# Two neighbouring heads, one in each half of the TensorE array and each with its own PSUM bank, in the attentions of a three-layer hybrid model

## The reference

```python
# window attention, per block of 128 queries
scores = jnp.einsum('bnqkgd,bnskd->bnkgqs', qb, kb).astype(jnp.float32) * (HEAD_DIM ** -0.5)
scores = jnp.where(mask[None, :, None, None], scores, -jnp.inf)
probs = jax.nn.softmax(jnp.concatenate([scores, sink], axis=-1), axis=-1)[..., :-1]

# forgetting attention, per block of 128 queries
cum = jnp.transpose(jnp.cumsum(log_f, axis=1), (0, 2, 1))
sc = jnp.einsum('bqhd,bkhd->bhqk', q[:, start:end], k[:, :end]).astype(jnp.float32) * scale
sc = sc + cum[:, :, start:end, None] - cum[:, :, None, :end]
sc = jnp.where(causal[None, None], sc, -jnp.inf)
probs = jax.nn.softmax(sc, axis=-1).astype(v.dtype)
```

## Time and profile before

| | us |
|---|---|
| median of 3 runs | 2251.22 |
| lowest and highest | 2249.53 and 2251.26 |
| the profiled execution | 2250.25 |
| its span | 2248.5 |
| TensorE busy | 2045.1 |
| VectorE busy | 1519.9 |
| ScalarE busy | 1106.0 |
| GpSimd busy | 90.9 |

### The profile page before, as it was taken

One profiled execution on the slowest core, in us unless ns is written; L12 is line 12 of the kernel. 1 busy time (PEld: TensorE's weight loads), 2 busy tenths in 40 slices (PEclk: granted clock), 3 DMA queues, 4 the chain that ended last, 5 costly groups with the idle time before them and its releaser, 6 DMA issues.

```text
span 2248.5 us, 25347 instructions
## 1 busy us (share of the span) xinstructions
PE 2045.1 (91%) x9466; PEld 1579.8 (70%) x9466; DVE 1519.9 (68%) x2305; ACT 1106.0 (49%) x1672; POOL 90.9 (4%) x85
## 2 busy tenths in 40 slices
PE   5998999998899999997689789876999999999996
PEld 4776777776777777776545445535888888888885
DVE  4967555555586845546846766326888888888885
ACT  4544545444453445444321012115777777777774
POOL 0000000000000000000002100001000000000000
PEclk9999999999899999998899899997999999999998
DMA  6533434344443443433444322253999999998994
GB/s 196 158 124 103 141 113 122 103 141 153 125 147 117 139 116 104 125 106 116 134 138 149 97 87 94 72 183 136 330 328 331 331 329 331 327 330 328 331 330 150
DMA packets 134602, 411.08 MB, mean 183 GB/s; under 512 B 17464, under 2 KB 19128, under 8 KB 107344
## 3 DMA queue, kind: packets, MB, share of 16 engines
q1 hardware_dynamic: 128480, 407.25, 53.9%
q0 software_dynamic: 6000, 2.22, 0.4%
HBM read 406.21 MB, written 19.45 MB: 189 GB/s over the span
## 4 chain that ended last, share of the span: by engine, by line
PE 76%; DVE 17%; ACT 4%; issue 2%; DMA 1%; SPq 0%; DVEq 0%; ACTq 0%; POOLq 0%
PE bank L588 17%; PE bank L589 16%; PE bank L590 16%; PE bank L636 9%; DVE r L1043 5%; DVE w_lo L1043 4%; PE bank L933 3%; PE bank L567 2%; PE bank L704 2%; PE bank L781 1%; PE bank L807 1%; PE bank L687 1%; PE bank L874 1%; DVE r L1049 1%; DVE r L1046 1%
## 5 line engine op out<-in xcount | busy, mean ns | idle before, releaser
L1043 DVE TENSOR_TENSOR w_lo<-w_raw,w_hi 128x1024 fp32r<-128x1024 f32 (+1 forms) x372 | 445.7, 1217 | 244.2 <-ACT w_hi L1875 235.6
L1875 ACT CAST w_hi<-w_raw 128x1024 fp32r<-128x1024 f32 (+1 forms) x266 | 277.8, 1047 | 187.6 <-PE bank L590 187.5
L588 PE MATMUL bank<-w_hi,h_hi 128*128 128x512 f32 x800 | 327.8, 410 | 12.9 <-DVE w_lo L1043 12.8
L589 PE MATMUL bank<-w_lo,h_hi 128*128 128x512 f32 x800 | 316.1, 395 | 0.0
L590 PE MATMUL bank<-w_hi,h_lo 128*128 128x512 f32 x800 | 315.7, 395 | 0.0
L588 PEld LDWEIGHTS bank<-w_hi,h_hi 128*128 128x128 f32 x800 | 153.4, 192 | 48.8 <-DVE w_lo L1043 14.1
L2031 ACT ACTIVATE r<-bank,small 128x256 f32<-128x256 f32 (+1 forms) x152 | 63.8, 424 | 243.2 <-DVE small L1046 243.1
L590 PEld LDWEIGHTS bank<-w_hi,h_lo 128*128 128x128 f32 x800 | 152.6, 191 | 33.7
L589 PEld LDWEIGHTS bank<-w_lo,h_hi 128*128 128x128 f32 x800 | 153.3, 192 | 29.5
L1043 DVE TENSOR_TENSOR w_lo<-r,w_hi 128x1024 fp32r<-128x1024 f32 x106 | 129.1, 1246 | 44.2 <-ACT w_hi L2140 44.1
L636 PE MATMUL bank<-w_raw,h_all 128*128 128x512 f32 (+1 forms) x320 | 142.3, 601 | 1.1 <-DVE h_all L1043 1.1
(11 more groups left out here) (320 smaller groups left out, 4125.7 us busy)
## 6 DMA issues: line engine op xcount, KB each, us to landing
w_raw<-in_w_in SPq DMA_DIRECT2D x236, 512.0 KB, 3.6
r<-in_w_up SPq DMA_DIRECT2D x69, 1024.0 KB, 5.2
w_raw<-in_w_gate SPq DMA_DIRECT2D x68, 1024.0 KB, 5.1
w_raw<-in_w_down SPq DMA_DIRECT2D x36, 1024.0 KB, 5.2
r<-in_w_down SPq DMA_DIRECT2D x34, 1024.0 KB, 5.1
w_raw<-in_w_proj SPq DMA_DIRECT2D x48, 512.0 KB, 3.7
w_raw<-in_w_out SPq DMA_DIRECT2D x24, 512.0 KB, 3.9
w_raw<-in_w_mem_kv SPq DMA_DIRECT2D x8, 512.0 KB, 3.6
```

The source lines that it names most:

```text
L588: e.matmul(out_, sh, mh, start=first, stop=False, skip_group_check=shared)
L589: e.matmul(out_, sh, ml, start=False, stop=False, skip_group_check=shared)
L1043: o.did(v.tensor_tensor(out_, a, b, op), sem, value)
L1875: a.copy(halves(n)[0], raw_of(n)).then_inc(w_hi, 1)
```

## The change

A unit is now heads h and h+1, so one head is in each half of the array. Each head's scores have a bank of their own, always 4 and 5 (`score_banks`); the turned probabilities always take 6 (`turn_bank`). `scores` is cut in two: `products`, for both heads, then `rest`, for the first and then the second head. The sum of forget gates runs over all 128 rows: `picks` is now zero from row 64 on, so the second copy of `cum` adds nothing. The banks are one tensor, so that VectorE can take the maximum of both banks by one instruction; ScalarE releases each bank behind its own exponential. The memory attention has no rest and only changes its banks.

```diff
+UNITS, UNITS_DSA, UNITS_MEM = ([(t, h) for t in range(T) for h in range(0, n, 2)] for n in (HEADS, 8, 4))
...
+        bank_all = ctx.enter_context(nc.psum_tensor("bank", [P, 8 * CH], F32))
+        banks = [bank_all[:, i * CH:(i + 1) * CH] for i in range(8)]
...
+            score_banks, turn_bank = Banks([4, 5]), Banks([6])
...
-                        b, bank = take(work, ("sc", tag, i))
+                        got = [take(score_banks, ("sc", tag, i, j)) for j in range(2)]
+                        last = [products(h0 + j, t, got[j][1][:, 0:keys], rest is None) for j in range(2)]
+                        if rest is not None:
+                            last = [rest(h0 + j, t, got[j][1][:, 0:keys]) for j in range(2)]
                         for j in range(2):
-                            done = scores(h0 + j * hs, t, bank[:, j * keys:(j + 1) * keys])
-                        done.then_inc(full[b], 1)
+                            last[j].then_inc(full[got[j][0]], 1)
                     if 1 <= i <= len(units):
                         t, h0 = units[i - 1]
                         n = 2 * keys_of(t) // P
-                        await_drained(("sc", tag, i - 1))
+                        for j in range(2):
+                            await_drained(("sc", tag, i - 1, j))
                         p = p_buf[(i - 1) % 2]
-                        b, bank = take(work, ("pt", tag, i - 1))
+                        b, bank = take(turn_bank, ("pt", tag, i - 1))
...
-                def scores(h, t, dst):
+                def products(h, t, dst, alone):
                     keys, par = (t + 1) * P, HD * (h % 2)
-                    e.matmul(dst, qT[par:par + HD, h // 2, t * P:(t + 1) * P], kT_c[par:par + HD, h // 2, 0:keys], start=True, stop=False)
-                    e.matmul(dst, picks[par:par + 64, h:h + 1].to_broadcast([64, P]), cum[par:par + 64, 0:keys], start=False, stop=False)
+                    return e.matmul(dst, qT[par:par + HD, h // 2, t * P:(t + 1) * P], kT_c[par:par + HD, h // 2, 0:keys], start=True, stop=alone)
+
+                def rest(h, t, dst):
+                    e.matmul(dst, picks[:, h:h + 1].to_broadcast([P, P]), cum[:, 0:(t + 1) * P], start=False, stop=False)
                     return e.matmul(dst[:, t * P:(t + 1) * P], idbf[:, :], causal_mask, start=False, stop=True)
...
+                        for j in range(2):
+                            await_full(("sc", tag, i, j))
                         c = t * heads + h0
-                        mx = mx_all[:, c:c + hs + 1:hs]
-                        o.did(v.tensor_reduce(mx, bank[:, 0:2 * keys_of(t)].rearrange("p (h k) -> p h k", h=2), AX, MAX))
+                        mx = mx_all[:, c:c + 2]
+                        two = bank_all[:, 4 * CH:6 * CH].rearrange("p (h k) -> p h k", h=2)
+                        o.did(v.tensor_reduce(mx, two[:, :, 0:keys_of(t)], AX, MAX))
...
                         for j in range(2):
-                            done = a.activation(p_buf[i % 2][:, j * keys:(j + 1) * keys], bank[:, j * keys:(j + 1) * keys], ACT.Exp,
-                                                bias=mx_all[:, c + j * hs:c + j * hs + 1], accum_out=sum_all[:, c + j * hs:c + j * hs + 1])
-                        done.then_inc(drained[b], 1)
+                            b, bank = await_full(("sc", tag, i, j))
+                            a.activation(p_buf[i % 2][:, j * keys:(j + 1) * keys], bank[:, 0:keys], ACT.Exp,
+                                         bias=mx_all[:, c + j:c + j + 1], accum_out=sum_all[:, c + j:c + j + 1]).then_inc(drained[b], 1)
...
-    c[:, 1250:1266] = i[:, None] % 32 == np.arange(16)
+    c[:, 1250:1266] = (i[:, None] % 32 == np.arange(16)) & (i[:, None] < 64)
```

More of the change, by code:

```diff
@@ L667, in dense, with attention @@
                         yield
-            def attention(tag, units, heads, dv, hs, keys_of, scores, v_of, p_buf, pT_buf):
+            def attention(tag, units, heads, dv, keys_of, products, rest, v_of, p_buf, pT_buf):
                 per_bank = min(CH // dv, heads)
@@ L777, in window @@
                 await_drained(("kT", l, 1))
-                def scores(h, t, dst):
+                def products(h, t, dst, alone):
                     keys, par = (t + 1) * P, HD * (h % 2)
-                    e.matmul(dst, qT[par:par + HD, h // 2, t * P:(t + 1) * P], kT_b[par:par + HD, h // KVH, 0:keys], start=True, stop=False)
+                    return e.matmul(dst, qT[par:par + HD, h // 2, t * P:(t + 1) * P], kT_b[par:par + HD, h // KVH, 0:keys], start=True, stop=alone)
+                def rest(h, t, dst):
                     return e.matmul(dst, idbf[:, :], causal_mask if t == 0 else window_mask, start=False, stop=True)
-                yield from attention(("b", l), UNITS, HEADS, HD, 2, lambda t: (t + 1) * P, scores,
+                yield from attention(("b", l), UNITS, HEADS, HD, lambda t: (t + 1) * P, products, rest,
                                      lambda h, b: kvb[:, b, 256 + (h // 4) * HD:256 + (h // 4 + 1) * HD],
@@ L856, in memory, with products @@
                 await_drained(("kTm", 1))
-                def scores(h, t, dst):
-                    return e.matmul(dst, qT_m[:, h, t * P:(t + 1) * P], kT_m[:, h, :], start=True, stop=True)
-                yield from attention("mem", UNITS_MEM, 4, 128, 1, lambda t: S, scores, lambda h, b: kmv[:, b, CH + h * 128:CH + (h + 1) * 128],
+                def products(h, t, dst, alone):
+                    return e.matmul(dst, qT_m[:, h, t * P:(t + 1) * P], kT_m[:, h, :], start=True, stop=alone)
+                yield from attention("mem", UNITS_MEM, 4, 128, lambda t: S, products, None, lambda h, b: kmv[:, b, CH + h * 128:CH + (h + 1) * 128],
                                      [R[9][:, 0:CH], R[9][:, CH:2 * CH]], [R[9][:, 2 * CH:3 * CH], R[9][:, 3 * CH:4 * CH]])
@@ L1284, in rope, with attention @@
                 o.prev()
-            def attention(tag, units, heads, dv, hs, keys_of, before, y3, stats_of, sink=None, gated=False):
+            def attention(tag, units, heads, dv, keys_of, y3, stats_of, sink=None, gated=False):
                 mx_all, sum_all = stats_of
@@ L1323, in finish @@
                 else:
-                    await_drained(("sc", tag, unit))
+                    for j in range(2):
+                        await_drained(("sc", tag, unit, j))
                 o.did(v.reciprocal(sm, sm))
@@ L1356, in window @@
                 await_drained(((("zb", l), 1), 1))
[L1357 removed]
+                yield from attention(("b", l), UNITS, HEADS, HD, lambda t: (t + 1) * P, y_b, att["b"], sink=sinks, gated=True)
                 yield
@@ L2018, in mamba, with attention @@
                 yield
-            def attention(tag, units, heads, dv, hs, keys_of, p_buf, pT_buf, stats_of, sink=False):
+            def attention(tag, units, heads, dv, keys_of, p_buf, pT_buf, stats_of, sink=False):
                 mx_all, sum_all = stats_of
```

42 lines of the change are left out of this document (18 added, 24 removed).

## The result

| | before | changed |
|---|---|---|
| median, us | 2251.24 | 2228.24 (2225.9 to 2229.79) |
| ratio to before | | 0.9899, 95% interval 0.9885 to 0.9913 |
| span of the profiled execution | 2248.5 | 2228.0 |

A forecast was written before the change was run, and what follows sets the result against it. TensorE was taken to bound the attention stages. Unit savings of 16 x 2.38 = 38.1 us, with +0.3 and +0.2 given back, took 2250.25 to 2212.7, or 2213.5 as median; range 2206 to 2229, forecast's chance 0.75.

The forecast's parts named there:

- The products of two halves overlap: Score products: two heads' products, one in each half, cost what one costs, 0.63 us at 256 keys, 0.42 at 128.
- Rival A: Score products: second head's first matmul does not pass first head's second; 10.9 us more, 2224 us; chance 0.09.
- Rival B: Score products: the halves do not overlap, only switches are saved; 20.8 us more, 2234 us; chance 0.05.
- Window units: Window attention, up to the turning: 0.54 us at 128 keys, saving 0.52; 0.87 at 256 keys, saving 0.72.
- mask to mask as before a turning: Step between a unit's two masks, without a trace row: booked at 0.06 and 0.12 us, bounds 0.05 and 0.16.
- the gate sum keeps its 0.06 and 0.12: Forget units: a gate sum over 128 rows costs as over 64, 0.06 us at 128 keys, 0.12 at 256.
- This margin does not shrink: Ahead of a unit's products: slack after the previous unit's exponential, 0.98 us at the tightest, stays, so waits cost nothing.
- rival C: Dense pieces come closer and wait for VectorE or ScalarE, or exponentials are late: at most 20 us back, 2218 to 2234; chance 0.07.
- Turnings have bank 6 alone and wait for the copy ..., a wait that stood behind them already: Turnings wait for the copy of the unit before, claimed to be no new wait; no size given.
- plus 0.2 to 0.5: Transposes of y_b in layer 0's forget stage: their first group meets the exponential wait instead of the second, costing 0.2 to 0.5 us.
- +0.2, bounds -3 and +3: Last stage's sparse and memory attention: gains of lone units and losses of pairs net to +0.2 us, bounds -3 and +3.
- I am wrong if the rows show the starts together and the span is not shorter by over 30 us: The prediction's own failure test: products of both heads start together, yet the span shortens by no more than 30 us.

The follow-up runs named there:

- Experiment 1: Changed kernel with the old choice of heads, h and h+2, both in the same half of the array: 2253.63 us, ratio 1.0004 to the kernel before.
- experiment 5: Changed kernel with both gate sums of a forget unit ahead of both masks, sums still over 128 rows: 2223.14 us, ratio 0.9883 to the kernel before.
- experiment 3: Changed kernel with gate sums over the 64 rows of the head's own half, between products and masks: 2223.35 us, ratio 0.9869 to the kernel before.
- experiment 7: Kernel before with only the fixed banks, scores in 4 and 5 in turn, turned weights in 6: 2257.44 us, ratio 1.0019.
- experiment 6: Changed kernel with gate sums over 64 rows and the third layer's attentions as before the change: 2220.2 us, and 2216.1 when run again.
- experiment 2: Changed kernel with each head's rest straight behind its product (product, rest, product, rest): 2281.87 us, ratio 1.0134 to the kernel before.

## Why the prediction was right, and where its sizes were off

- **The products of two halves overlap: right.** 0.64 for four instructions, 0.007 us between the heads. Experiment 1 takes the overlap away, and 18.5 of the 27.4 us gained in the first two layers go with it. Rival A would have put the second head's first product behind the first head's second, 0.3 later; the Trainium skill's rule behind it, "TensorE: Matmul & The Clock Gate", Part 3 ("The mechanism"), that matmuls start in program order, is contradicted here by a second kind of work beside the indexer's. Rival B is experiment 1, not this kernel.
- **Window units, "0.42 + 0.06 + 0.06" and "0.63 + 0.12 + 0.12": right.** Saved 0.51 and 0.73 a unit, 19.8 us over both layers. The bound "mask to mask as before a turning" held: 0.066 and 0.119.
- **Forget units: the term "the gate sum keeps its 0.06 and 0.12" failed.** At full height a gate sum takes 0.16 and 0.22 to its mask (mean of the two heads); the step from a mask to a gate sum, booked at 0.11, takes 0.04. Together 0.13 and 0.12 a unit, 4.0 us. Counting columns alone was the mistake. They are the same, and with its weights loaded ahead a full-height sum of 256 columns does take 0.12 (experiment 5's second); but behind the products, and behind a mask, the load over all rows no longer runs ahead (experiments 3 and 5).
- **"This margin does not shrink": true ahead of the products, false elsewhere.** No unit of the two stages waits there. But I read margins on TensorE's queue and only for the exponential. The window's last turning (1.19 us of wait), the one product with the values that waits for VectorE to empty bank 7 (0.57 of wait, 0.74 of delay) were within reach of a TensorE that runs 9 us ahead of VectorE's dense work. The window stages should have shortened by 9.9 each; they shortened by 8.0 and 7.6. Of the 4.2 us that are missing these two waits, in both layers, hold 2 x (1.19 + 0.74) = 3.9. That is rival C at a small size, which I had given 0.07 as a case of its own, where it is a cost that comes on top of the forecast.
- **"Turnings have bank 6 alone and wait for the copy ..., a wait that stood behind them already": wrong by 0.45 us in this place** (the copy ends after both exponentials), and free at the old length of a unit (experiment 7).
- **y_b's transposes, "plus 0.2 to 0.5" in layer 0:** 0.98 us of wait for the exponential became 1.58, and layer 1, which I had left out, went from 1.0 to 1.84, there for the copy. With 0.2 and 0.1 more for `y_lo` behind it, 1.7 us against 0.3.
- **The third layer, net "+0.2, bounds -3 and +3":** the mechanism was right (first pair: second scores 3.2 us behind the first, 3.0 forecast), the size 1.2 us by the waits, 2.4 by all profiles with the clock's share in it, 6.3 in the first comparison. The first two lie within the bounds. What I had no term for is the clock.

My own test was "I am wrong if the rows show the starts together and the span is not shorter by over 30 us". They do and it is not, so by it the sum was wrong. Its terms, put right: the net 37.6 less 4.0 (gates), 4.2 (window stages), 1.4 (y_b) and 2.2 (third layer) is 25.8. Measured were 23.0 in the first comparison of medians and 24.7 in the second (2252.27 less 2227.57). With the gate sums over 64 rows and the old third layer (experiment 6) the time is 2216 to 2220, a gain of 32 to 36 us. The 1 to 3 us that no term holds lie within what the half clock shifts from one execution to the next; that they are its doing is argued, not shown.

That the range held is in part luck. I gave 0.75 to the sum, whose bounds end at 2220, and the result lies 8 us above them, in the stretch of rival C, to which I had given 0.07; one of its four executions, 2229.79, is outside the range as well. The chances of the faster cases add up to 0.96, not 0.95.

## What to carry to other kernels

Put products of the two halves of the array next to each other, with all that can stay at half height between them, and what needs all rows behind: a sum over 128 rows right behind the halves took 0.22 us here instead of 0.12, as its weights were not loaded ahead. Two such sums in a row are better than each with a mask behind it (experiment 5), and sums at half height between the products and the masks better still (experiment 3). When one engine's queue is shortened, check the margins against what the other engines do that is not shortened, at the ends of stages above all. Before a difference of a few microseconds in one stage is explained, take a second profile of both kernels and look at the clock.

## What the runs showed of the chip that I had not expected

- TensorE interleaves products of two halves against program order, yet lets none pass an instruction over all rows (0.007 us between the heads' products, and 1.01 in experiment 2).
- The half clock (1.2 GHz) falls in different places in executions of one program. The version of experiment 6, twice, same forget stage of layer 0, first and second profile (clock is the last column but two):

```profile
392.00:402.00 10.00, 9.21 (x36) 6.66 (x36) 3.90 (x5) 4.07 (x10) 0.52 (x1) 0.66 0.27 79
```
```profile
392.00:402.00 10.00, 7.73 (x48) 5.92 (x49) 5.11 (x10) 4.38 (x10) 0.52 (x1) 1.00 0.31 88
```

From its first dense product to its last this stage took 139.90 us in the first, with 13.7 us of it at half, and 134.26 in the second, with none: 0.4 us lost for each us at half. In the first, the clock fell at 393.5, 0.8 us behind TensorE's wait of 1.7 us for y_b; in the second the same wait is there, with no fall. What decides between the two stays open.
